# A fused encoder layer on one core: TensorE's wait for its own last unit at the end of each weight group is taken out, and the readers of a group wait for the unit counter instead

## The reference, cut to what matters

```
h  = rms_norm(x);  z = h @ W_in                      # 12296 columns: q, k, v, gates of two mixers
yA = forgetting_attention(q, k, v, log_f) @ W_a_up   # 8 heads x 128
yB = hgrn2_recurrence(q, k, v, log_f) @ W_b_up       # 8 heads, 128 x 128 state
x  = x + (sigmoid(gA) * yA + sigmoid(gB) * yB) @ W_o
h2 = rms_norm(x);  q = h2 @ W_q;  scores = q . keys  # top 16 of 128 x 128 experts per head
x  = x + sum over chosen experts of gate * gelu(h2 . U[e]) * V[e]
out = rms_norm(x)
```

## Time and profile before

| what | value |
|---|---|
| median of three runs | 2100.49 us |
| the profiled execution's own time | 2100.55 us |
| its span, first to last instruction | 2098.8 us |
| TensorE busy | 1454.3 us (69%) |
| VectorE busy | 1614.9 us (77%) |
| ScalarE busy | 870.8 us (41%) |
| GpSimd busy | 1005.9 us (48%) |
| mean granted TensorE clock | 0.837 |
| HBM read | 598.29 MB |

### The profile page before, as it was taken

One profiled execution on the slowest core, in us unless ns is written; L12 is line 12 of the kernel. 1 busy time (PEld: TensorE's weight loads), 2 busy tenths in 40 slices (PEclk: granted clock), 3 DMA queues, 4 the chain that ended last, 5 costly groups with the idle time before them and its releaser, 6 DMA issues.

```text
span 2098.8 us, 22990 instructions
## 1 busy us (share of the span) xinstructions
PE 1454.3 (69%) x8113; PEld 1262.1 (60%) x8113; DVE 1614.9 (77%) x2023; ACT 870.8 (41%) x1131; POOL 1005.9 (48%) x699
## 2 busy tenths in 40 slices
PE   6999999999999999920000001211358999999997
PEld 6987998877778789820000001211347888888886
DVE  5465765455745556689999989977888999999998
ACT  4353432344333444211221126577855434444444
POOL 1002220000000000168888878888877768888883
PEclk9999999999999999965555555555569999999998
DMA  6555433434555554789999999999946999999996
GB/s 209 175 179 187 155 126 138 163 134 155 178 181 183 197 181 161 261 305 422 422 414 414 419 402 388 420 421 422 418 160 241 358 362 367 378 394 381 383 372 245
DMA packets 151804, 601.83 MB, mean 287 GB/s; under 512 B 14720, under 2 KB 14736, under 8 KB 118288
## 3 DMA queue, kind: packets, MB, share of 16 engines
q0 software_dynamic: 58048, 364.41, 43.3%
q1 hardware_dynamic: 93648, 236.02, 31.8%
HBM read 598.29 MB, written 2.10 MB: 286 GB/s over the span
## 4 chain that ended last, share of the span: by engine, by line
PE 54%; issue 15%; DVE 13%; POOL 9%; DMA 6%; ACT 1%; DVEq 0%; POOLq 0%; SPq 0%; ACTq 0%; PEldq 0%
PE acc L1665 8%; PE acc L1667 7%; PE acc L1666 7%; POOL slots L524 6%; DVE slots L1435 4%; PE acc L1648 4%; PE acc L1651 4%; PE acc L1650 4%; PE acc L1976 3%; DMA slots<-in_peer_u,expert 3%; PE acc L1977 3%; PE scr L1977 3%; PE acc L1978 3%; PE scr L1976 3%; PE scr L1978 3%
## 5 line engine op out<-in xcount | busy, mean ns | idle before, releaser
L916 DVE TENSOR_TENSOR w_lo<-raw,w_hi 128x2048 fp32r<-128x2048 f32 x136 | 314.7, 2315 | 295.8 <-ACT w_hi L585 294.8
L1435 DVE SCALAR_TENSOR_TENSOR slots<-slots,acc 128x2048 f32<-128x2048 f32 x188 | 424.7, 2285 | 46.6 <-DMA slots<-in_peer_u,expert 44.3
L585 ACT ACTIVATE w_hi<-raw 128x2048 fp32r<-128x2048 f32 x136 | 260.3, 1915 | 428.2 <-PE acc L1667 286.0
L569 POOL DMA_INDIRECT starts<-in_v_gather,expert x256 | 376.5, 1471 | 103.0 <-DVE X L1567 54.4
L524 POOL DMA_INDIRECT slots<-in_peer_u,expert x256 | 252.7, 987 | 256.7 <-DVE expert L1407 147.1
L532 POOL TENSOR_TENSOR slots<-slots,N 128x2048 f32<-128x2048 f32 x62 | 280.7, 4527 | 32.3 <-DMA slots<-in_peer_u,expert 32.1
L878 ACT ACTIVATE v_hi<-v_raw 128x1344 fp32r<-128x1344 f32 x128 | 170.4, 1332 | 277.8 <-PE scr L1978 192.9
L779 ACT ACTIVATE slots<-slots 128x2048 f32<-128x2048 f32 x62 | 118.5, 1911 | 355.6 <-POOL slots L532 355.6
L1567 DVE SCALAR_TENSOR_TENSOR X<-starts,weight,X 128x704 f32<-128x704 f32 x256 | 243.1, 950 | 17.8 <-DMA starts<-in_v_gather,expert 7.0
L1946 PE MATMUL scr<-hot_a,hot_b 128*128 128x128 f32 x384 | 84.6, 392 | 220.7 <-DVE hot_b L1483 151.8
L1665 PE MATMUL acc<-w_hi,hT_hi 128*128 128x512 f32 x576 | 228.7, 397 | 5.1 <-PE acc L1667 3.6
(11 more groups left out here) (289 smaller groups left out, 3214.3 us busy)
## 6 DMA issues: line engine op xcount, KB each, us to landing
raw<-in_w_in SPq DMA_DIRECT2D x88, 1024.0 KB, 4.9
v_raw<-in_v_dense SPq DMA_DIRECT2D x128, 672.0 KB
raw<-in_w_o SPq DMA_DIRECT2D x16, 1024.0 KB, 5.1
raw<-in_peer_wq SPq DMA_DIRECT2D x16, 1024.0 KB, 5.1
raw<-in_w_a_up SPq DMA_DIRECT2D x8, 1024.0 KB, 5.1
raw<-in_w_b_up SPq DMA_DIRECT2D x8, 1024.0 KB, 5.0
slots<-in_peer_u,expert POOLq DMA_INDIRECT x256, 9.3
starts<-in_v_gather,expert POOLq DMA_INDIRECT x256
```

What stands on the lines that cost most here:

```text
L569: pool.indirect_dma_start(starts[j][:, :], None, v_gather[:, :], bass.IndirectOffsetOnAxis(ap=expert[:, s // NSEL, s % NSEL:s % NSEL + 1], ...
L585: a.activation(w_hi[:, m % 2, :, :], raw[:, m % 2, :, :], ACT.Copy).then_inc(hi_ready, 1)
L916: v.tensor_tensor(w_lo[:, m % 2, :, :], raw[:, m % 2, :, :], w_hi[:, m % 2, :, :].bitcast(fp32), ALU.subtract).then_inc(lo_ready, 1)
L1435: v.scalar_tensor_tensor(out=slots[j][:, :], in0=slots[j][:, :], scalar=1.0, in1=row, op0=ALU.mult, op1=ALU.mult, accum_out=hid_sum[:, t, ...
```

## The change

The wait and the increment at each group's end are taken out of TensorE's queue, `group_done` goes away, and each reader waits until `unit_done` has reached the number of units up to the end of its group, which is the same event. No operation on data changes on any engine, and no instruction changes its place.

```diff
-        unit_done, group_done = sem("unit_done"), sem("group_done")
+        unit_done = sem("unit_done")
...
                 if q == 0:
-                    pool.wait_ge(group_done, G_WQ)
+                    pool.wait_ge(unit_done, UNIT0[G_WQ])
                 if q == 2 * FOUR:
-                    pool.wait_ge(group_done, G_END)
+                    pool.wait_ge(unit_done, UNIT0[G_END])
...
             def gate_a(n):
 
-                act.wait_ge(group_done, G_GA + n + 1)
+                act.wait_ge(unit_done, UNIT0[G_GA + n + 1])
...
             def copy_group(g, to):
 
-                dve.wait_ge(group_done, g + 1)
+                dve.wait_ge(unit_done, UNIT0[g + 1])
...
             def add_residual(n):
-                dve.wait_ge(group_done, G_WO + n + 1)
+                dve.wait_ge(unit_done, UNIT0[G_WO + n + 1])
...
-            def finish(g, i=0, per=0):
-
-                pe.wait_ge(unit_done, UNIT0[g + 1] + i * per)
-                pe.sem_inc(group_done, 1)
-
             def loop_two(g0, unit, src, split=None):
...
                             unit(g, m, src, i, 2 * n)
-                        finish(g, i, 2 * n)
```

More of the change, by code:

```diff
@@ L711, in _ @@
                 group(G_GB + 2 * n + 1)
-                act.wait_ge(group_done, G_GB + 2 * n + 1)
+                act.wait_ge(unit_done, UNIT0[G_GB + 2 * n + 1])
                 act.wait_ge(gb_used, 1 + n)
@@ L1233, in times_ya @@
             def times_ya(n):
-                dve.wait_ge(group_done, G_AUP + n + 1)
+                dve.wait_ge(unit_done, UNIT0[G_AUP + n + 1])
                 dve.wait_ge(ga_ready, n + 1)
@@ L1273, in add_yb @@
             def add_yb(n):
-                dve.wait_ge(group_done, G_GB + 2 * n + 2)
+                dve.wait_ge(unit_done, UNIT0[G_GB + 2 * n + 2])
                 dve.wait_ge(gb_ready, n + 1)
@@ L1709, in _ @@
             transposed_unit(G_HQF, 3, hT)
-            finish(G_HQF)
             for g in range(G_HQF + 1, G_HIG):
@@ L1713, in _ @@
                     transposed_unit(g, m, hT)
-                finish(g)
             loop_two(G_HIG, natural_unit, hT)
@@ L1733, in _ @@
                     transposed_unit(g, m, hT)
-                    if m == 3:
-                        finish(g)
                     if m % 2:
@@ L1758, in _ @@
             natural_unit(G_FV, 3, hT)
-            finish(G_FV)
             level_products("diagonala", k_hg, q_hg, 0, own)
@@ L1783, in _ @@
             natural_unit(G_FV + 1, 3, hT)
-            finish(G_FV + 1)
             def logits(pair):
@@ L1875, in _ @@
                 natural_unit(g + 1, 1, (ob_hi, ob_lo))
-                finish(g + 1)
                 if n < 2:
@@ L1887, in _ @@
                     transpose_merged(3)
-            finish(G_WO)
             for g in range(G_WO + 1, G_WQ):
```

## The result

| | before | after |
|---|---|---|
| median of runs on one chip | 2101.14 us (2095.09 to 2103.11, 6) | 2078.47 us (2072.34 to 2084.63, 6) |
| after over before, 95% interval | | 0.9891 [0.9873, 0.9910] |
| profiled execution | 2100.55 us | 2078.43 us |
| span of it | 2098.8 us | 2076.7 us |
| first gather | 859.86 us | 839.64 us |

The sign and the mechanism are as forecast.

What follows compares the result with a forecast made beforehand. TensorE sets the pace to about 825 us, gathers of U from 930 to 1540. Transposed ends 3.9, natural 8.5, loops 3.9, readers 0.1: 16.4 us off 2100.55 gives 2084.2 us; 8-in-10 range 2080.5 to 2091.

Steps and rivals of the forecast that it cites:

- The sign and the mechanism: Faster, since TensorE no longer empties its array at groups' ends; chance of faster by over 0.2%: 0.90.
- 0.1 for the readers: Copies out of `acc` wait for one semaphore, not two; on the path only at GpSimd's ninth gather, 0.1 us.
- The loop steps: Loop ends: three between groups at 0.6, two exits at 0.65, second loop's jump back and next end 0.8: 3.9 us.
- the term for the natural ends: Outside the loops: nine ends at 0.54 us to natural units or G_WQ, 4.9 us; seven at 0.47 to small work, 3.3.
- the low part's margin of the earlier trace: At G_WO ends the next unit's low part was ready 0.59 us early, against a gain of 0.47: just holds.
- The six ends at nothing: Before the first loop, its jump back, last G_GB, inside G_WQ, last group: a later wait or no following work, no gain.
- The clock term: Low clock stretches of 1.6 us each behind logits or the late load: change taken as nothing, 1.6 us to each side.
- slower: Rival: with the rests gone, low clock comes more often in 208 to 819 us; 2105 us, chance 0.03.
- from there the span is the old one shifted: Last G_WQ matmul, first and ninth gather all about 16 us earlier, the rest unchanged behind them.
- Short price: Rival: an end is worth only 0.18 us, the rest belongs to a group's first matmul; 2094.8 us, chance 0.06.
- nothing: Rival: the step is all the group's start, or another wait is the true last one; 2100.5 us, chance 0.06.
- the clock rival: Rival: more or longer low clock stretches, behind the logits and around 880 us; 2088.8 us, chance 0.15.

Runs made afterwards that it cites:

- late start: Kernel after with three more 1 MB loads ahead of all others on SyncE, so TensorE's first unit starts 15.4 us later: 2095.07 us, ratio 0.9974.
- Five thin ends: Kernel after with wait and increment kept only at five ends, from the second of G_FV to the last of G_GA: 2085.25 us, ratio 0.9954.
- wait without increment: Kernel after with TensorE's wait for its last unit put back at each group's end, without the increment: 2090.48 us, ratio 0.9964.
- all ends but G_WQ's: Kernel after with wait and increment kept at all groups' ends but the four of G_WQ: 2098.49 us, ratio 1.0002.
- after again: Kernel after run once more, word for word, nothing changed: 2078.97 us, ratio 0.9925.
- in mid-group: Kernel after with wait and increment put behind each group's first unit, not its last: 2096.12 us, ratio 0.9980.
- five free ends: Kernel after with wait and increment kept at five ends forecast at nothing (last transposed G_HQF, last G_GB, last three G_WQ): 2076.38 us, ratio 0.9905.

## Why the prediction was right in its mechanism and wrong in its size

**The price of an end held, to a few tenths.** Profiles with the ends in (in one of them all but G_WQ's) have a "plain" of 833.6, 833.4, 835.0 and 832.9 us, those without 817.0, 817.7, 817.6, 817.5 and 817.7: means 833.7 and 817.5, a difference of 16.2 us, or 16.7 with the slow start taken out. The sum of the prediction without its 0.1 for the readers was 16.3. Its terms moved a little against each other: the loop steps were wholly won (0.65 each was taken for the exits; 1.02 - 0.23 = 0.79 was there), and the term for the natural ends was a little too large, since the four G_WO ends gave 0.46, 0.58, 0.47 and 0.24 us and not 0.54 each: the low part's margin of the earlier trace rows ran out at the last. The readers' 0.1 is below what "plain" can tell. The prediction put the whole step down to the emptying of the array; about a third of it goes with the increment.

**The places where a gain stops held.** The six ends at nothing are nothing, five of them by an experiment. At the place of the earlier trace rows the wait was forecast at one unit, and it came at two, since the low part of the unit ahead was late as well.

**The step that failed: "I leave it at nothing, with 1.6 us to each side".** The clock term was not nothing. Four profiles with the ends in have 4, 5, 4 and 4 low stretches ahead of the first gather; four without have 2, 1, 1 and 2. That is 2.75 fewer on average, 4.5 us; with late start's 3 it is 2.45 fewer, 4.0 us. The prediction saw that low stretches stand behind thin work, with a `finish` in front; it then argued about the shift of time, by which a stretch could be won or lost evenly, and only in its rival "slower" about the rests, where it said that fewer rests have nothing to trigger. It did not turn this round: with a rest in front of it TensorE does still less around thin work, and taking the rest away may take stretches away. "Five thin ends" speaks for this, with the rests put back at those places alone: five stretches, and a median that is higher by more than the waits. The granted clock there is 1.2 GHz, half of the full 2.4. It is not shown beyond doubt. How the rest brings the stretch about no run shows; "late start", without rests, has three, and "wait without increment", with shorter rests at every end, has two, so the length of the rest or the moment at which thin work comes has a part in it. No run varied either by itself.

**The second step that failed: "from there the span is the old one shifted".** Between the first and the ninth gather the kernel gains another 4 to 5 us, since a load lands up to 4 us earlier against the first gather and the wait for it, with the low stretch behind, goes. What makes it land earlier is open. In before and after the load and the first five gathers are issued at the same distance from the first gather (3.63 us for the load). That it is the absolute time is ruled out by "late start"; that it is G_WQ's waits alone is ruled out by "all ends but G_WQ's" (42.2 us). The numbers between the extremes suggest that both sets of ends play a part.

**What the medians say of the whole.** Profile against profile the three parts are 16.2 + 4.5 + 4.8 (44.0 to 39.2 us over the same eight profiles), 25.5 us at the ninth gather, and those eight profiled times differ by 26.5 us (means 2102.1 and 2075.6). The medians differ by less, 19.5 to 24.3 us by the comparison taken: kernels with all ends in stand at 2098.4 to 2101.1 and those without at 2076.4 to 2079.0. By the recorded ratios it is 22.9 us in the main comparison (18.9 to 26.7) and 15.7 in after again (10.9 to 20.6). Executions of one program lie up to 14 us apart, and the gathers of U alone vary by 8 us between two profiles of before. So 16 to 17 us are shown. Of the other 9 that the profiles show, 3 to 8 reach the medians, and by the ratio of after again none, or up to 4; how many are the clock's and how many the load's, the timings can't part. The 2 us by which the time lies below the range are fewer than this uncertainty; that two terms were wrongly put at nothing does not hang on them, since the profiles show both.

**The rivals.** "Short price" and "nothing" are refuted by the rows and by "in mid-group". "Slower" and the clock rival had the clock term and gave it the wrong sign. The Trainium skill, TensorE: Matmul & The Clock Gate, "Single matmul latency", gives a lone matmul a constant of 166 ns over its columns at the full clock. That is no figure for a wait, and the prediction's estimate of 5.3 us for the 32 ends, made from it, falls short for a wait alone as well: the runs show 0.29 to 0.35 us, about twice that.

## What to carry to other kernels

TensorE waiting for its own last result pays for the wait (here 0.3 us) and for an increment behind it (0.2 us at a group's end, 0.06 in mid-group); where others can wait for a counter that the work raises anyway, both go at no cost. Count such a wait only where no wait close behind it hangs on a chain that starts at the last unit's end and so does not see what was removed. And where the granted clock falls behind thin work, look whether a rest stands in front of it, and price the stretches as a term of their own, with a sign.

## What the runs showed of the chip

- At a group's end a wait of TensorE for its own last matmul costs 0.21 to 0.22 us in the first step and 0.11 in the second; an increment behind it raises the first to 0.46 to 0.47 and leaves 0.07 in the second. In mid-group wait and increment cost 0.31 and 0.07 to 0.08. With the wait already met, the two cost nothing.
- A loop's jump back or exit costs TensorE no step (0.23 us, as any other) with no wait ahead of it; behind the wait and the increment the exit's step was 1.02 us.
- In one profile each, five rests of 0.5 us ahead of thin work went with three stretches more at the lower clock than the two of "five free ends", each of which cost 1.65 us; rests of 0.33 us at every end went with two as well.
- The same program can start at either rate: the matmuls of after's first unit stood 0.12 us apart, and those of after again 0.21 until 23.4 us, which moved the second unit by 0.9 us.
- A load of 1 MB, issued 3.3 to 4.3 us behind the first gather of 1 MB, let ScalarE start between 12.2 and 17.9 us after that gather, and between 12.2 and 17.1 in the ten profiles that issue it 3.6 us behind; the page's median for such loads is 5.1 us to landing.
- In all thirteen profiles the clock fell between the first and ninth gather when a wait of TensorE for a unit there was over 2.7 us (seven), and stayed full when none was over 1.7 us (six).
